# Expert tokens gathered by number from rows stored once, and state-space step sizes by four column quarters, in a three-block layer stack on one core

## What is computed

```python
# second block, state-space mixer: 16 step sizes a token
dt_raw = (x @ w_in_2)[..., 6144:6160]
dt = softplus(dt_raw + dt_bias)            # once forwards, once backwards
# third block, mixture of experts: 32 experts in 4 groups, 2 experts a token
experts = (g_idx * 8 + top_i).reshape(-1)  # 512 tokens x 2
for e in range(32):                        # dropless: every chosen token is computed
    hid = silu(x[tok_e] @ w_gate[e]) * (x[tok_e] @ w_up[e])    # 1024 -> 512
    y[tok_e] += weight * (hid @ w_down[e])                     # 512 -> 1024
x = layer_norm(2**0.25 * x + y, ln3_g, ln3_b)
```

## Time and profile before

| | |
|---|---|
| median of 3 runs | 3171.22 us (3164.98 to 3174.51) |
| profiled execution | 3166.15 us, its span 3164.5 us |
| PE busy | 2992.5 us, 95% of the span |
| DVE, ACT, POOL busy | 45%, 23%, 4% |
| mean granted PE clock | 0.968 |
| DMA | 420.48 MB, mean 133 GB/s |

### The profile page before, as it was taken

The page is one execution under the profiler, slowest core; times in us unless marked ns, Lnnn a source line. Parts: engine busy times, 40 slices in busy tenths (PEclk is TensorE's granted clock), DMA queues, the critical chain, the costliest instruction groups (busy, mean ns, idle before and its releaser), DMA issues. The chain is left out here.

```text
span 3164.5 us, 38490 instructions
## 1 busy us (share of the span) xinstructions
PE 2992.5 (95%) x15072; PEld 2139.5 (68%) x15072; DVE 1423.0 (45%) x2507; ACT 723.1 (23%) x1702; POOL 123.5 (4%) x149
## 2 busy tenths in 40 slices
PE   7999999999999899988999999999989987999996
PEld 4577757888878678877788887877766643333332
DVE  3554325344353768367543354425744232333335
ACT  0331113220011653661100001115531222111111
POOL 1000000000000210000100001000100001000000
PEclk9999999999999999998999999998889988999998
DMA  9122122222222012101232222222012209999995
GB/s 376 68 80 80 54 86 79 81 87 80 102 64 77 27 55 80 54 1 43 78 103 84 80 96 91 80 83 81 2 68 80 69 0 413 423 424 424 422 425 214
DMA packets 129894, 420.48 MB, mean 133 GB/s; under 512 B 6705, under 2 KB 35778, under 8 KB 108242
## 3 DMA queue, kind: packets, MB, share of 16 engines
q1 hardware_dynamic: 121842, 379.48, 31.3%
q10 hardware_dynamic: 3024, 23.59, 1.8%
q0 software_dynamic: 4880, 15.35, 1.4%
HBM read 394.81 MB, written 23.59 MB: 132 GB/s over the span
## 5 line engine op out<-in xcount | busy, mean ns | idle before, releaser
L770 PE MATMUL bank<-arena 128*128 128x256 f32 x5152 | 1122.2, 380 | 11.7 <-ACT spare L921 3.4
L770 PEld LDWEIGHTS bank<-arena 128*128 128x128 f32 x5152 | 979.5, 190 | 151.5 <-issue 7.3
L1081 PE MATMUL bank<-arena 128*128 128x256 f32 x1652 | 364.0, 383 | 10.0 <-PEq L131 3.5
L1081 PEld LDWEIGHTS bank<-arena 128*128 128x128 f32 x1652 | 317.4, 193 | 55.4 <-issue 11.5
L178 PE MATMUL bank<-arena 128*128 128x512 f32 (+6 forms) x652 | 218.6, 491 | 19.3 <-PEq L1480 5.7
L178 PEld LDWEIGHTS bank<-arena 128*128 128x128 f32 (+1 forms) x652 | 115.8, 196 | 117.9 <-issue 99.5
L383 PE MATMUL bank<-arena 128*128 128x512 f32 x384 | 166.0, 593 | 4.5 <-PEq L1693 2.0
L4065 DVE TENSOR_TENSOR arena<-arena,bank 128x512 f32<-128x512 f32 x128 | 87.7, 687 | 138.6 <-PE bank L3970 136.3
L383 PEld LDWEIGHTS bank<-arena 128*128 128x128 f32 x384 | 72.5, 190 | 94.7 <-issue 94.7
L834 DVE TENSOR_TENSOR arena<-arena 128x1024 f32<-128x1024 f32 x46 | 56.3, 1224 | 175.9 <-PE bank L770 171.8
L3942 PE MATMUL bank<-arena 128*32 128x512 f32 x1024 | 117.8, 602 | 14.5 <-DMA arena<-in_moe_w_up_dram 14.5
(11 more groups left out here) (586 smaller groups left out, 3474.1 us busy)
## 6 DMA issues: line engine op xcount, KB each, us to landing
arena<-in_moe_w_gate_dram SPq DMA_DIRECT2D x64, 1024.0 KB, 17.0
arena<-in_moe_w_up_dram SPq DMA_DIRECT2D x64, 1024.0 KB, 19.1
arena<-in_moe_w_down_dram SPq DMA_DIRECT2D x32, 2048.0 KB, 24.3
arena<-in_w_in_dram SPq DMA_DIRECT2D x29, 2048.0 KB, 8.0
arena<-in_w_ff_dram SPq DMA_DIRECT2D x16, 2048.0 KB, 7.8
x_slots<-arena ACTq DMA_DIRECT2D x8, 2048.0 KB, 32.8
arena<-in_w_out_dram SPq DMA_DIRECT2D x8, 2048.0 KB, 7.8
arena<-in_w_gate_dram SPq DMA_DIRECT2D x11, 1024.0 KB, 5.3
```

Of the source, the lines that this page charges most:

```text
L770: last = pe.matmul(bank[:, m, :], lhsT, rhs, start=fresh and m == 0 and k == 0, stop=k == 3, skip_group_check=True)
L1081: last = pe.matmul(bank[:, m, :], x[:, k, m * P:(m + 1) * P], w[:, k, :], start=opening and m == 0 and k == 0, stop=k == w.shape[1] - 1, s ...
```

## The change

Two independent parts. In the first, SP stores the rows of x once, in token order, in `x_rows` (512 rows, 2.1 MB), in the block before the experts. DVE and PE form a table that has for each pair the token number of each of its 128 slots: eight matmuls with a one-hot of the slot in its pair as stationary operand and, streaming, a one-hot of the pair times the token's number (33 columns). For each pair DVE picks the next column (`find_tokens`, four small instructions) and POOL gathers the rows from `x_rows` by an indirect DMA. An empty slot names token 0. `x_slots`, its clearing, the scatter and the cast of the slot numbers are gone. Expert 0 always gets a large chunk (the clamp of `larges[:, 0:1]`), so the large expert of pair 0 is known beforehand, and its weights (6.3 MB) are loaded in the block before, where they lie in other units than before; the number of pairs stays 16.

In the second part, the 16 step-size columns are widened to 32 (the last 32 of the weight), which are the stationary operand, and xT streams through in 512 columns; the 8 feature chunks are spread over four column quarters of the array, two in each. ACT copies the 128x512 result to SBUF, and four matmuls against four stacked 16x16 identities (made by POOL) add the quarters and turn the result to token rows. They stand after product 1 of the first chunk.

```diff
 # setup_constants
-            pool.memset(zeros, 0.0).then_inc(zeroed.sem, zeroed.up())
...
-            act.wait_ge(zeroed.sem, zeroed.at(1))
-            clear_slots(c, act, zeros)
 # first_block, tables
-        pool.wait_ge(c.signals["slots_cleared"].sem, c.signals["slots_cleared"].sent)
 # plan_second
-            c.plan("dt2", w[:, :, 6144:6160])
+            c.plan("dt2", w[:, :, 6128:6160])
 # state_space, PE
-            for i in range(NT):
-                for k in range(KD):
-                    last = pe.matmul(c.banks[4][:, i * SH:(i + 1) * SH], xT[:, k, i * P:(i + 1) * P], w[:, k, :],
-                                     start=i == 0 and k == 0, stop=k == KD - 1, skip_group_check=True)
+            for k in range(2):
+                for q in range(4):
+                    last = pe.matmul(c.banks[4][32 * q:32 * q + 32, :], w[:, 2 * q + k, :], xT[:, 2 * q + k, :],
+                                     start=k == 0, stop=k == 1, tile_position=(0, 32 * q))
             last.then_inc(dt_made.sem, dt_made.up())
             c.release("dt2", dt_made)
+            sevens.one(pe, 0, 1)
+            pe.wait_ge(dt_copied.sem, dt_copied.at(1))
+            pe.wait_ge(made.sem, made.at(3))
+            for i in range(NT):
+                last = pe.matmul(c.banks[6][:, i * SH:(i + 1) * SH], dt_parts[:, i * P:(i + 1) * P], dt_rows, start=i == 0,
+                                 stop=True, skip_group_check=True)
 # state_space, ACT, ahead of heads.squares(act)
+            act.wait_ge(dt_made.sem, dt_made.at(1))
+            act.activation(dt_parts, c.banks[4][:, :], ACT.Copy).then_inc(dt_copied.sem, dt_copied.up())
 # Router.transfers (new), on SP in the block before the experts
+        for half in range(2):
+            for n, (dst, name) in enumerate(((gate, "moe_w_gate_3"), (up, "moe_w_up_3"))):
+                k = slice(half * KD // 2, (half + 1) * KD // 2)
+                sync.dma_start(dst[:, k, :], self.a[name][0][0].rearrange("(p k) n -> p k n", p=P)[:, k, :]).then_inc(
+                    self.landed[0][3 * half + n].sem, 16)
+        sync.dma_start(down, self.a["moe_w_down_3"][0][0].rearrange("(p k) n -> p k n", p=P)).then_inc(
+            self.landed[0][2].sem, 16)
+        for i in range(NT):
+            sync.wait_ge(self.reordered.sem, self.reordered.at(i + 1))
+            sync.dma_start(self.x_rows[i * P:(i + 1) * P, :], self.rows[i]).then_inc(self.stored.sem, self.stored.up(16))
 # expert_pairs, POOL
-            for n in range(2):
-                for i in range(NT):
-                    pool.indirect_dma_start(
-                        out=c.x_slots, out_offset=bass.IndirectOffsetOnAxis(ap=slot_i[:, n, i:i + 1], axis=0),
-                        in_=rows[i], in_offset=None).then_inc(scattered.sem, 16)
-            pool.wait_ge(scattered.sem, scattered.at(16 * 2 * NT))
-            pool.dma_start(tokens, c.x_slots[PAIR:2 * PAIR, :]).then_inc(tokens_landed.sem, 16)
+            def gather(count, before):
+                pool.wait_ge(found.sem, count)
+                pool.wait_ge(asked.sem, before)
+                pool.tensor_tensor(route.asked, c.ones[:, 0:1], c.ones[:, 0:1], ALU.add).then_inc(asked.sem, 1)
+                pool.indirect_dma_start(out=tokens, out_offset=None, in_=route.x_rows,
+                                        in_offset=bass.IndirectOffsetOnAxis(ap=route.token_i, axis=0)).then_inc(
+                                            tokens_landed.sem, 16)
+            gather(1, asked.at(0))
             with pool.Fori(0, more) as it:
                 pool.wait_ge(turns_done.sem, it * 2 + 4)
-                pool.dma_start(tokens, c.x_slots[bass.ds((it + 2) * PAIR, PAIR), :]).then_inc(tokens_landed.sem, 16)
+                gather(it + 2, it + asked.at(1))
 # expert_pairs, PE, between the slot numbers' rows and the first gate and up products
+            pe.wait_ge(spread_out.sem, spread_out.at(3))
+            for n in range(2 * NT):
+                last = pe.matmul(up_bank[:, 0:MAX_PAIRS + 1], by_slot[:, n, :], by_pair[:, n, :], start=n == 0,
+                                 stop=n == 2 * NT - 1)
+            last.then_inc(tabled.sem, tabled.up())
+            pe.wait_ge(found.sem, 1)
 # expert_pairs, DVE: once before the loop and once in each trip, after copy_tokens
+            def find_tokens(n):
+                dve.wait_ge(tokens_landed.sem, n * 16 + 16)
+                ...
+                dve.scalar_tensor_tensor(out=route.chosen_pair, in0=iota[:, 0:MAX_PAIRS + 1], scalar=route.next_pair,
+                                         in1=route.token_table, op0=ALU.is_equal, op1=ALU.mult).then_inc(stepped.sem, 1)
+                dve.tensor_reduce(route.found, route.chosen_pair, AX.X, ALU.add).then_inc(stepped.sem, 1)
+                dve.tensor_scalar(route.next_pair, route.next_pair, 1.0, None, ALU.add).then_inc(stepped.sem, 1)
+                dve.tensor_copy(route.token_i, route.found).then_inc(found.sem, 1)
```

More of the change, by code:

```diff
@@ L2520, in state_space @@
     neg = [small[:, 1600:1728], small[:, 1728:1856]]
+    dt_rows, dt_parts, dt_copied = small[:, 1856:1856 + SH], c.spare[:, 0:S], c.sig("turned_copied")
     conv, made, got = c.sig("conv_ready"), c.sig("iota_made"), c.sig("rows_loaded_gpsimd")
@@ L2525, in tables @@
     def tables(pool):
+        part = lambda q: c.ident[:, 32 * q + SH:32 * q + 2 * SH]
+        pool.tensor_tensor(dt_rows, part(0), part(1), ALU.add).then_inc(made.sem, made.up())
+        for q in (2, 3):
+            pool.wait_ge(made.sem, made.sent)
+            pool.tensor_tensor(dt_rows, dt_rows, part(q), ALU.add).then_inc(made.sem, made.up())
         for n, k in enumerate(("dt_bias_fwd_2", "dt_bias_bwd_2", "a_log_fwd_2", "a_log_bwd_2", "d_skip_2")):
@@ L3505 @@
 MAX_PAIRS = 32
-def clear_slots(c, act, zeros):
-    cleared = c.sig("slots_cleared")
-    c.x_slots = c.nc.dram_tensor("x_slots", ((MAX_PAIRS + 1) * PAIR, D), F32).ap()
-    room = c.x_slots.rearrange("(p r) n -> p (r n)", p=P)
-    for at in range(0, room.shape[1], UNIT):
-        n = min(UNIT, room.shape[1] - at)
-        act.dma_start(room[:, at:at + n], zeros[:, 0:n]).then_inc(cleared.sem, cleared.up(16))
 class Router:
@@ L3531, in __init__ @@
         self.iota, self.before, self.row, self.steps = take(P), take(P), take(1), take(5)
+        self.pair_ends, self.token_no = take(MAX_PAIRS), take(NT)
         self.weights, self.count = take(KD, 40), take(NE)
@@ L3541, in __init__ @@
                                "exponentials", "experts_listed", "experts_turned"))
+        first = 2 + len(c.chunks) % RING
+        ring = [2 + (first - 2 + n) % RING for n in range(RING)]
+        self.gate_w = [c.region(unit, 0, KD, FFE) for unit in (5, 1)]
+        self.up_w = [c.region(unit, 0, KD, FFE) for unit in (6, ring[1])]
+        self.down_w = [c.region(unit, 0, FFE // P, D) for unit in (ring[0], ring[2])]
+        self.landed = [[c.sig(f"{n}_weights_landed{s}") for n in ("gate", "up", "down", "gate_second_half",
+                                                                  "up_second_half")] for s in range(2)]
+        self.x_rows = c.nc.dram_tensor("x_rows", (S, D), F32).ap()
+        self.stored = c.sig("result_written")
         self.order, self.made, self.got = (c.sig(n) for n in ("vector_order_aside", "iota_made", "rows_loaded_gpsimd"))
@@ new lines, in number_slots, with pair_tokens @@
+        dve.wait_ge(numbered.sem, numbered.sent)
+    def pair_tokens(dve, spread_out):
+        order = c.sig("vector_order")
+        flat = slots.rearrange("p n i -> p (n i)")
+        dve.tensor_tensor(past, flat.unsqueeze(2).to_broadcast([P, 2 * NT, MAX_PAIRS]),
+                          route.pair_ends.unsqueeze(1).to_broadcast([P, 2 * NT, MAX_PAIRS]),
+                          ALU.is_ge).then_inc(order.sem, order.up())
+        dve.wait_ge(order.sem, order.sent)
+        dve.tensor_reduce(pair_of, past, AX.X, ALU.add).then_inc(order.sem, order.up())
+        dve.wait_ge(order.sem, order.sent)
+        dve.scalar_tensor_tensor(out=slots_in.rearrange("p n i -> p (n i)"), in0=pair_of, scalar=float(-PAIR), in1=flat,
+                                 op0=ALU.mult, op1=ALU.add).then_inc(order.sem, order.up())
+        dve.tensor_tensor(by_pair, route.iota[:, 0:MAX_PAIRS + 1].unsqueeze(1).to_broadcast([P, 2 * NT, MAX_PAIRS + 1]),
+                          pair_of.unsqueeze(2).to_broadcast([P, 2 * NT, MAX_PAIRS + 1]),
+                          ALU.is_equal).then_inc(order.sem, order.up())
+        dve.wait_ge(order.sem, order.sent)
+        for n in range(2):
+            half = by_pair[:, n * NT:(n + 1) * NT, :]
+            dve.tensor_tensor(half, half, route.token_no.unsqueeze(2).to_broadcast([P, NT, MAX_PAIRS + 1]),
+                              ALU.mult).then_inc(spread_out.sem, spread_out.up())
+        dve.tensor_tensor(by_slot, route.iota.unsqueeze(1).to_broadcast([P, 2 * NT, P]),
+                          slots_in.rearrange("p n i -> p (n i)").unsqueeze(2).to_broadcast([P, 2 * NT, P]),
```

(19 more changed lines are left out.)

67 lines of the change are left out of this document (44 added, 23 removed).

## The result

The changed kernel takes 3146.34 us (median of 4 runs, 3145.72 to 3148.36), the kernel before 3171.13 (4 runs, 3164.98 to 3174.51): a ratio of 0.9926, 95% interval 0.9912 to 0.9940. The prediction was 3145, range 3131 to 3160. The profiled execution took 3145.72 with a span of 3143.8, so 20.7 us of span less than before's 3164.5. The kernel before has one run more here than in its table of times, where the median was 3171.22.

A forecast was written before the change was run, and what follows sets the result against it. PE was taken to bound the state-space block and the DMA's weight stream the expert loop. 3166.15 - 1.1 - 9.2 - 13.0 = 3142.9 us for the profiled execution, 3147.9 from the median; forecast 3145, range 3131 to 3160.

The forecast's parts named there:

- Start: Program start: without ACT's nine clearing DMAs the first block ends with DVE, 1.1 us sooner; bounds 0 to 2.
- Step sizes: Head of the state-space block: quarters, product 1 and turning take 8.3 us instead of 17.5, 9.2 less; bounds 6.8 to 11.3.
- Expert part: Expert block: fewer bytes in the saturated stream, restarted later, end the last weight wait 13.0 us sooner; bounds 8 to 15.
- the stream runs from 2645.2: Expert loop: weight transfers restart 1 us after the first load leaves at 2644.2, then 454.8 us of bytes follow.
- about the ninth: Expert loop: the pair from which PE, at 30.0 us a trip against the DMA's 31.0, waits for loads again.
- No second hole: Expert loop after pair 0: the DMA queue stays full to 2676, while PE frees pair 1's first half at about 2671.
- trips of 31.0: Expert loop: from about the ninth pair the DMA sets the trip at 31.0 us, with one PE wait.
- gather like a load: Expert loop: a pair's indirect gather costs the DMA the same as a token load, 1.24 us of all engines.
- Bytes alone count: Rival, expert part: the stream runs on in 2630 to 2645, gaining 24.8 us there, 35 in all; 3131 to 3136, chance 0.06.
- the hole: Expert block: the DMA stands near zero for some 15 us from about 2630, until PE frees a weight slot.
- The gather is slower: Rival, expert loop: repeated reads of one row hold the DMA, paid 15 times; at 4 us each 3184 us, chance 0.06.
- Part of it is given back: Rival: PE's trip exceeds 30.65 us or DVE's sums eat the state-space gain; 10 to 15 us in all, 3151 to 3161, chance 0.12.

The follow-up runs named there:

- no_early_load: The changed kernel with pair 0's large expert (6.29 MB) loaded at the head of the expert block as before: 3145.70 us, ratio 0.9924 to the kernel before.
- plain_rows: The changed kernel with each pair's token gather replaced by a plain load of 128 neighbouring stored rows: 3146.42 us, ratio 0.9923 to the kernel before.
- one_token: The changed kernel with every slot's token number set to 0, so each gather reads one row 128 times: 3145.73 us, ratio 0.9923 to the kernel before.

## Why the prediction was right, and where not

The start of PE's second block in the kernel after, which answers to the earlier trace rows:

```profile
20.83 4.08 PE L178 MATMUL bank<-arena 128*128 128x512 f32 x5 [4.46 <-PEq L1481]
```

- **Start, -1.1.** PE's second block began at 20.83 instead of 21.95, 1.12 sooner. But three more traces with ACT's clearing began between 20.44 and 23.12, since the first block itself moves by that much. PE's wait ahead of this block is 4.5 us in the traces without the clearing and 5.1 to 6.0 in those where ACT clears, so the term is 0.6 to 1.6 us. When PE reached the state-space block the kernel after was 2.75 us ahead. The other 1.6 us are no part of the change: 1.1 of them is a clock that rose sooner (0.83 against 0.66 from 20 to 30 us), and in other traces it rose sooner with the clearing than without it. Over all traces the state-space block begins at 1136.9 to 1139.5 where ACT clears (four, mean 1138.2) and at 1135.7 to 1138.3 without (nine, mean 1136.8): 1.4 us. That the 17.3 MB cost PE nothing holds.
- **Step sizes, -9.2 (6.8 to 11.3).** Measured 10.94. The mechanism was right and the size 1.7 off. The term of the sum that was mis-sized is product 1: it was put at 5.2 us because the clock should fall and return as before; the fall never came, and it took 3.7. The quarters took 1.93 (1.9 forecast), the turning 0.96 (1.2). The Trainium skill, "TensorE: Matmul & The Clock Gate", section "Why this matters for your kernels", would have had the quarters 0.4 us dearer; 1.93 goes with the row. The waits were hidden as argued: behind the block's first matmul PE has no wait up to 1190 us in the profile, so ACT's copies cost it nothing.
- **Expert part, -13.0 (8 to 15).** Measured 10.5. The table's delay was 1.96 us (2.0 forecast), the one-hots took 3.1 under the picks (3.5), and the loop's first load left 32.67 us after the block's (2644.2 - 2611.53 = 32.7 forecast). The step that failed is the next, "the stream runs from 2645.2", together with an end put at the last byte. The 165 GB/s of 2630 to 2640 are 3.9 us of 423, so counted at the full rate the stream ran from 2636.1, 1.8 us after the load and not 1.0 (bytes moved from 2635 on, but at 147 and 205 GB/s until 2637); and 454.8 us of bytes from there end at 3090.9, the wait at 3092.6. These 1.7 us I had left out on one side only: the same count for the kernel before, 210.7 MB from 2612.5, ends at 3110.7, and its wait at 3112.97. The Trainium skill, "DMA: Bandwidth & Descriptors", section "Anatomy of one DMA — SWDGE (gpsimd) path", gives a DMA that GpSimd issues a fixed cost of about 2.0 us, most of it the wait for the receipt of the last byte. The weights here are issued by SP, of which that section does not speak; the two distances, 1.7 and 2.3 us, are of that size, though no row splits them. PE waited from pair 3 on and not from "about the ninth": by my own numbers the loads were some 4.5 us ahead of PE at pair 1 and lost 1.0 a trip, which makes the sixth, and 2.5 us less make the third.
- **No second hole, trips of 31.0, gather like a load.** All three hold, the first two by the profile (419 GB/s or more in each ten microseconds from 2640 to 2700, 30.95 us a trip), the last by two experiments.
- **The rivals.** *Bytes alone count* fell with the hole in the profile and with no_early_load. *The gather is slower* fell with plain_rows and one_token. *Part of it is given back* did not happen in the loop: DVE's search and the gather left the trip at 31 us. What the prediction did not say, though its own count had it, is that the early load is worth nothing as long as the hole stands.
- **The sum** of the span: 2.75 + 10.94 + 10.5 + 0.4 (tail) are 24.6; 3.9 went back in unchanged code, of which C's 5.2 us are the largest piece. The forecast did not know of that lottery. Its hit on the median to 1.3 us is in part luck: 2.5 us too much for the expert part stand against 1.7 too little for the step sizes, and the 5 us lost in C against the 5 by which the profile of before lay under its median.

## What to carry to other kernels

When a loop is bound by a stream of loads into slots that compute sets free, the bytes ahead of the loop do not matter as long as they are through before the first slot is free; find the instruction that frees the first slot, and count everything on that engine ahead of it at full price. A transfer taken out of the saturated stretch is a gain only if it would have been there: here 4.2 MB of scatter were, and 6.3 MB of weights were not. A change of some tenths of a percent in a kernel with a clock that comes and goes is better read from distances inside the trace than from medians, after two or three traces of the kernel before have shown which distances stand still. Where a distance moves, look at the granted clock beside it, and compare traces with the same one.

## What the runs showed of the hardware

- A stretch of unchanged matmuls, 1800 of them, took 180.9, 183.5, 186.1 or 188.6 us, with granted clocks of 0.84, 0.83, 0.81 and 0.82 over it.
- The 128x16 matmuls of the step sizes, with PE busy 5.00 of 5.00 us, had a granted clock of 0.54 from 1140 to 1145 and 0.50 from 1145 to 1150 in the kernel before; the same sums as 128x512 in four quarters had 1.00, and so did the work behind them.
- An indirect DMA of 128 rows of 4 KB took no more of the stream than a plain load, with all rows the same too: 458.3, 458.4 and 458.3 us from the loop's first load to the last wait.
- Four column quarters of 128x512 took 1.93 us for 16 passes and 3.64 us for 32, where two 64-column halves side by side take 0.43 us for one pass of each.
- From the first load's issue after a pause to the stream, counted back from its bytes at 423 GB/s, it took 1.0 us at the block's start (kernel before) and 1.8 at the loop's (kernel after).
- The 17.3 MB of clearing, at some 400 GB/s beside PE's matmuls, left 180 passes at 72.12 to 72.14 us, as without them.
